# A two-layer gated-convolution, pooling and gating decoder step with experts: gate products ordered further ahead of their branch, small TensorE steps moved between blocks, another prologue and another item head

## The reference

```python
for i in range(2):
    xn = rmsnorm(x, norm_mix_g[i])
    z = xn @ w_in[i]                       # 8 x 256 mixer columns, then 4 x 1024 gate columns
    br_a = B(z) * conv3(C(z) * h(z))
    br_b = silu(layernorm(conv31(cfa(z) * sigmoid(cfb(z))) + bias))
    br_c = (pool_2_4_8_16(zp) - zp) @ pool_w * scale
    br_d = u(z) * (tril(sgu_w) @ layernorm(v(z)) + sgu_b)
    proj = [br @ w_branch[i, n] for n, br in enumerate((br_a, br_b, br_c, br_d))]
    x = x + (sum(sigmoid(gate_n(z)) * proj[n] for n in range(4))) @ w_out[i]
    xn = rmsnorm(x, norm_ffn_g[i])
    x = x + (swiglu(xn) if i == 0 else top2_of_8_swiglu_experts(xn))
    x = x + sigmoid(rmsnorm(x, norm_ple_g[i]) @ ple_w_gate[i]) * (p[i] @ ple_w_proj[i])
y = rmsnorm(x, final_norm_g)
```

## Time and profile before

| | us |
|---|---|
| median of 3 runs | 5181.46 (5172.38 to 5184.09) |
| the profiled execution | 5169.23 |
| its span, first to last instruction | 5167.6 |
| PE busy | 4955.4 (96%) |
| DVE busy | 3402.1 (66%) |
| ACT busy | 1598.1 (31%) |
| POOL busy | 402.1 (8%) |
| mean granted clock of TensorE | 0.975 |

### The profile page before, as it was taken

How to read it: one execution, slowest core, us unless ns; L and a number is a source line. 1 busy time by engine, 2 the same in 40 slices (tenths; PEclk the granted TensorE clock), 3 DMA queues, 4 the chain that set the end, 5 groups by cost and what they waited for, 6 DMA issues and landing times. The chain is left out here.

```text
span 5167.6 us, 86722 instructions
## 1 busy us (share of the span) xinstructions
PE 4955.4 (96%) x33128; PEld 4885.8 (95%) x33129; DVE 3402.1 (66%) x5297; ACT 1598.1 (31%) x2280; POOL 402.1 (8%) x246
## 2 busy tenths in 40 slices
PE   8999999999998999999969999999999999999979
PEld 7999999999998999999959999999999999999968
DVE  5677756445546656776556776666667887876665
ACT  2111222111112311122224444333334444443333
POOL 3111101101012021111010000000000000000020
PEclk8999999999999999999979999999999999999979
DMA  2111111111111111111035554444445555554431
GB/s 96 51 38 39 43 48 33 50 42 47 41 49 43 42 45 50 40 41 46 31 114 170 179 170 167 156 146 148 159 154 196 194 191 181 199 176 155 146 124 42
DMA packets 398927, 527.51 MB, mean 102 GB/s; under 512 B 12056, under 2 KB 353606, under 8 KB 398616
## 3 DMA queue, kind: packets, MB, share of 16 engines
q1 hardware_dynamic: 359552, 460.75, 26.7%
q0 software_dynamic: 11136, 33.97, 2.0%
q10 hardware_dynamic: 27928, 28.60, 1.7%
HBM read 494.87 MB, written 28.39 MB: 101 GB/s over the span
## 5 line engine op out<-in xcount | busy, mean ns | idle before, releaser
L1522 DVE TENSOR_TENSOR WLO<-WRAW,WHI 128x1024 fp32r<-128x1024 f32 x866 | 1065.7, 1232 | 316.3 <-ACT WHI L1138 189.7
L661 PE MATMUL PS<-XHI,WHI 128*128 128x384 f32 (+1 forms) x3648 | 1201.8, 329 | 0.6 <-DVE XLO L1749 0.3
L663 PE MATMUL PS<-XHI,WLO 128*128 128x384 f32 (+1 forms) x3648 | 1196.8, 328 | 0.0
L662 PE MATMUL PS<-XLO,WHI 128*128 128x384 f32 (+1 forms) x3648 | 1196.3, 328 | 0.0
L1138 ACT ACTIVATE WHI<-WRAW 128x1024 fp32r<-128x1024 f32 x866 | 898.9, 1051 | 885.4 <-PE PS L767 610.4
L661 PE MATMUL PS<-XSH,WHI 128*128 128x232 f32 (+6 forms) x3584 | 1059.8, 296 | 24.6 <-DVEq L2201 21.3
L662 PE MATMUL PS<-XSL,WHI 128*128 128x232 f32 (+6 forms) x3584 | 1057.0, 295 | 0.0
L663 PE MATMUL PS<-XSH,WLO 128*128 128x232 f32 (+6 forms) x3584 | 1055.5, 295 | 0.0
L661 PEld LDWEIGHTS PS<-XSH,WHI 128*128 128x128 f32 x3584 | 681.5, 190 | 26.7 <-DVE EACC L2249 22.9
L661 PEld LDWEIGHTS PS<-XHI,WHI 128*128 128x128 f32 x3648 | 690.7, 189 | 2.8 <-DVE XLO L1749 1.0
L662 PEld LDWEIGHTS PS<-XLO,WHI 128*128 128x128 f32 x3648 | 690.7, 189 | 0.7
(11 more groups left out here) (367 smaller groups left out, 5775.7 us busy)
## 6 DMA issues: line engine op xcount, KB each, us to landing
WRAW<-in_moe_w_gate SPq DMA_DIRECT2D x112, 1024.0 KB, 4.9
WRAW<-in_moe_w_up SPq DMA_DIRECT2D x112, 1024.0 KB, 4.9
WRAW<-in_moe_w_down SPq DMA_DIRECT2D x112, 1024.0 KB, 4.9
WRAW<-in_w_in SPq DMA_DIRECT2D x48, 1024.0 KB, 5.2
WRAW<-in_ffn_w_gate SPq DMA_DIRECT2D x11, 1024.0 KB, 5.1
WRAW<-in_ffn_w_up SPq DMA_DIRECT2D x11, 1024.0 KB, 5.2
WRAW<-in_ffn_w_down SPq DMA_DIRECT2D x11, 1024.0 KB, 4.8
XG<-sorted_rows POOLq DMA_DIRECT2D x18, 512.0 KB, 4.9
```

The costliest lines, as they stand in the source:

```text
L661: pe.matmul(PS[:, bank, 0:n], wh, hi(k), start=(k == 0), stop=False)
L662: pe.matmul(PS[:, bank, 0:n], wh, lo(k), start=False, stop=False)
L663: ins = pe.matmul(PS[:, bank, 0:n], wl, hi(k), start=False, stop=(k == KC - 1))
L1522: v.do(dve.tensor_tensor(WLO[s][:], raw_view(conv.n // 2 % RAW, conv.n % 2, kind), WHI[s][:].bitcast(F32), ALU.subtract), conv)
```

## The change

1. **Gates ahead.** In the first of the eight steps of every `gate_project`, TensorE computes the gates of all three blocks, then waits for the branch, then computes the three branch products. DVE and ACT follow: three gate tiles T[0] to T[2], then three additions. The other seven steps stay alternating.
2. **Small steps behind a block.** `column_unit` and `gate_project` take a list `between`. State stores, channel sums, pool weights, the transposes of p (layer 0), `stats` and `spread` stand behind the first or second block of a unit instead of ahead of it or behind the whole of it.
3. **Waits by slice and block.** Where a unit follows newly split activations, it waits for each slice of each block. The split of XNEW at the end of layer 0 is in 24 pieces, block by block, instead of 8.
4. **Prologue.** The gain rows are issued by ACT's queue and transposed ahead of everything. The squares are no longer added in the bank-wise order: ACT squares the token rows of XIN with a running sum into RTOK (nine operations of 1024 elements), after the first two conversions. `stats()` is left out for layer 0's first norm. The first unit waits for a block's evictions and not for the sums; the spread follows the first block of the second unit.
5. **Item head.** The first unit of an item waits slice by slice and stands ahead of the aligned address; a second unit at 336 tokens follows behind it, and then the jump. The bodies begin with the third unit.

```diff
-        def column_unit(HI, LO, first_use=None, after_first=lambda: None):
-
-            use()
+        def blocks_of(HI, LO, splits=None, between=()):
+
             slot = unit.n % HL
-            for t0, n in BLOCKS:
+            for j, (t0, n) in enumerate(BLOCKS):
                 b = open_bank()
                 product(b, n, slot, lambda k: HI[:, k, t0:t0 + n], lambda k: LO[:, k, t0:t0 + n],
-                        first_use if t0 == 0 else None).then_inc(q.next(), 1)
-                if t0 == 0:
-                    after_first()
+                        (lambda k: splits(j, k)) if splits else None).then_inc(q.next(), 1)
+                if j < len(between):
+                    between[j]()
...
+            for d in range(KC):
+                use()
+                slot = unit.n % HL
+                if d == 0:
+                    blocks_of(XHI, XLO, splits, between)
+                    pe.wait_ge(S[ready], count)
+                    pe.wait_ge(S["pw_lo"], pw.n + 1)
+                    for t0, n in BLOCKS:
+                        branch(t0, n)
+                else:
                     for t0, n in BLOCKS:
                         b = open_bank()
                         product(b, n, slot, lambda k: XHI[:, k, t0:t0 + n], lambda k: XLO[:, k, t0:t0 + n]).then_inc(q.next(), 1)
...
-            stats()
-            column_unit(XHI, XLO, first_use=(W_MIX1 if l else None))
-            spread()
-            column_unit(XHI, XLO)
+            if l:
+                column_unit(XHI, XLO, splits=lambda j, k: W_MIX1 + KC * j + k + 1, between=(stats, spread))
+                column_unit(XHI, XLO)
+            else:
+                use()
+                slot = unit.n % HL
+                for j, (t0, n) in enumerate(BLOCKS):
+                    pe.wait_ge(S["evicted"], KC * (j + 1))
+                    b = open_bank()
+                    product(b, n, slot, lambda k: XHI[:, k, t0:t0 + n], lambda k: XLO[:, k, t0:t0 + n]).then_inc(q.next(), 1)
+                unit.n += 1
+                column_unit(XHI, XLO, between=(spread,))
...
-            states_out(GLU, YB, PB)
-            gate_project("br_d", l + 1, U_SPLIT)
+            gate_project("br_d", l + 1, U_SPLIT, between=(lambda: states_out(GLU, YB, PB),))
...
+            column_unit(XHI, XLO, between=(channel_sums,))
...
-            states_out(ZP, YP, PC)
-            gate_project("br_b", l + 1, YB_SPLIT)
+            column_unit(XHI, XLO, between=(spread,))
+            gate_project("br_b", l + 1, YB_SPLIT, between=(lambda: states_out(ZP, YP, PC),))
...
+            gate_project("br_c", l + 1, YP_SPLIT, between=(pool_weights,))
...
                             if first and u == 0:
-                                spread()
+                                column_unit(XHI, XLO, splits=lambda j, k: W_FFN - 3 * KC + 3 * k + j + 1, between=(stats, spread))
...
                     nc.switch_bb("item_announced")
+                    splits = hs.n
+                    hs.n += KC
+                    gate_up(CAP, lambda k: hs.at(splits + k + 1))
                     pe.addr_align(256, offset=0, max_nops=0)
-                    pe.wait_ge(S["split_done"], hs.take(KC))
                     gate_up(CAP)
...
-                            left = item(rows, 1, fetch_next)
+                            left = item(rows, 2, fetch_next)
...
+            if l == 0:
+                last_down = W_FFN + 6 * FFN_GROUPS
+                gate_project("p_ready", 1, P_SPLIT, splits=lambda j, k: last_down + 3 * k + j + 1,
+                             between=(lambda: (p_columns(), stats()), spread))
+            else:
+                p_columns()
+                gate_project("p_ready", 2, P_SPLIT, splits=lambda j, k: hs.at(hs.n + min(6 * j + 6, 2 * NT)), between=(stats, spread))
...
+        act.wait_ge(S["rtok_clear"], 1)
+        for block, (t0, n) in enumerate(BLOCKS):
+            tiles = range(t0 // P, -(-(t0 + n) // P))
+            act.wait_ge(S[f"x_loaded{block}"], 16 * len(tiles))
+            for j in tiles:
+                w = tokens(j)
+                act.activation(XIN[0:w, j, :], XIN[0:w, j, :], ACT.Square, accum_out=RTOK[0:w, j:j + 1]).then_inc(S["row_squares"], 1)
+        convert()
...
             for d in range(KC):
                 convert()
                 if merge and 1 <= d <= MERGE_EARLY:
                     merge_low(d - 1)
-                for j, (t0, n) in enumerate(BLOCKS):
+                if d == 0:
+                    three = [gates(d, j, br_pulls) for j in range(3)]
+                for j in range(3):
                     if j == 2 and d < KC - 1:
                         split_pw()
...
+                    add_branch(d, j, *(gates(d, j, br_pulls) if d else three[j]))
```

More of the change, by code:

```diff
@@ L698, in _, with gate_project, branch @@
         sq, diag = Count(), Count()
-        def gate_project(ready, count, Y, after_first=lambda: None):
-            pe_ready = [False]
-            for j in range(4):
-                for h in range(2):
-                    use()
-                    slot = unit.n % HL
+        def gate_project(ready, count, Y, splits=None, between=()):
+            def branch(t0, n):
+                b = open_bank()
+                wh, wl = PWH[pw.n % 2], PWL[pw.n % 2]
+                for k in range(2):
+                    pe.matmul(PS[:, b, 0:n], wh[:, k, :], Y[0][:, k, t0:t0 + n], start=(k == 0), stop=False)
+                    pe.matmul(PS[:, b, 0:n], wh[:, k, :], Y[1][:, k, t0:t0 + n], start=False, stop=False)
+                    ins = pe.matmul(PS[:, b, 0:n], wl[:, k, :], Y[0][:, k, t0:t0 + n], start=False, stop=(k == 1))
+                ins.then_inc(q.next(), 1)
+            for d in range(KC):
[8 more added lines that the diff above has]
+                else:
                     for t0, n in BLOCKS:
@@ L869, in _, with pool_weights @@
-            gate_project("br_c", l + 1, YP_SPLIT)
+            column_unit(XHI, XLO, between=(spread,))
+            gate_project("br_b", l + 1, YB_SPLIT, between=(lambda: states_out(ZP, YP, PC),))
+            def pool_weights():
+                pe.wait_ge(S["pooled"], l + 1)
+                pe.wait_ge(S["pbd_loaded"], 64 * (l + 1))
+                for c in range(2):
+                    for t0, n in BLOCKS:
+                        b = misc_bank()
+                        pe.matmul(PS[:, b, 0:n], PBD[:, c, :], YP[:, c, t0:t0 + n], start=True, stop=True).then_inc(m.next(), 1)
@@ L1482, in _ @@
                         act.activation(x, x, ACT.Copy, scale=gain(6)[:, d:d + 1]).then_inc(S["xnew_ready"], 1)
+                for j, (t0, n) in enumerate(BLOCKS):
+                    if j == 2 and d < KC - 1:
+                        split_pw()
+                    sigmoid(n, d, j)
+                    q.n += 2
+                    if d:
+                        squares(t0, n)
+                if d == 0:
+                    for t0, n in BLOCKS:
+                        squares(t0, n)
             if l == 0:
-                for d in range(KC):
-                    act.wait_ge(S["split_req"], split.at(split.n + 1))
-                    act.activation(XHI[:, d, :], XNEW[:, d, :], ACT.Copy).then_inc(split.next(), 1)
+                for t0, n in BLOCKS:
+                    for d in range(KC):
+                        act.wait_ge(S["split_req"], split.at(split.n + 1))
+                        act.activation(XHI[:, d, t0:t0 + n], XNEW[:, d, t0:t0 + n], ACT.Copy).then_inc(split.next(), 1)
         norm_sqrt()
@@ L1753, in _ @@
                 dve.sem_inc(S["sgu_zeroed"], 1)
-            norm()
+                norm()
+            else:
+                norm_rows()
+                diagonals()
+                convert()
+                spread_rstd()
             v.do(dve.memset(MV[:], 1.0))
@@ L2347, in _ @@
                     v.sync()
-                    split_x(d, j, x, low=False)
+                    return x
+                if d == 0:
+                    three = [gates(d, j) for j in range(3)]
+                    whole = []
+                    for j in range(3):
+                        if j == 2:
+                            split_pw()
+                        whole.append(add_gated(j, *three[j]))
+                    for j in range(3):
+                        split_x(d, j, whole[j], low=False)
+                else:
+                    for j in range(3):
+                        if j == 2 and d < KC - 1:
+                            split_pw()
+                        gate = gates(d, j)
+                        finish_x()
+                        split_x(d, j, add_gated(j, *gate), low=False)
             finish_x()
```

219 lines of the change are left out of this document (104 added, 115 removed).

## The result

The changed kernel takes 5144.59 us (median of 4 runs, 5142.14 to 5149.72); the kernel before took 5182.77 us on the same chip (5172.38 to 5188.36). The ratio is 0.993, 95% interval 0.9912 to 0.9948: faster by 36 us (38 by the medians). The forecast was 68 us, 5113 us with a range from 5085 to 5138. The sign was right, the size was half, and the time lies above the range.

What follows compares the result with a forecast made beforehand. TensorE, busy 96% of the span, bounds the kernel; only its idle time or lower clock can yield. Terms 14 + 27 + 3.3 + 5 + 1 - 1 + 18.6 = 68 us, so 5181.5 - 68 = 5113 us, range 5085 to 5138.

Steps and rivals of the forecast that it cites:

- prologue: Start of the kernel: first product at 31.0 us instead of 44.98, a gain of 14 us (9 to 19).
- small steps and gates ahead: Mixers, both layers: waits at state stores, branches, channel sums and pool weights covered, plus clock: 27 us together.
- FFN entry: Statistics wait goes behind the first block: 3.3 us gained (1 to 6).
- the layer embedding of layer 0: A gate block moves into the wait for copies of P, and a low-half weights wait is covered: 5 us (3 to 9).
- entry to layer 1: Split of x in 24 pieces: gain of 3 us against a delay of 2 to 5, -1 us (-4 to 2).
- item heads: Slice waits at seven heads: 15.5 us of idle and 7.5 of clock, less 4.4 for the wider unit; 18.6 (8 to 26).
- last layer embedding: Layer embedding of layer 1: 1.5 us of waits go, the clock may fall once; +1 us (-2 to 3).
- So I put no new stall there: First unit of gate stages: about 13 us of DVE work against 15 of TensorE, six banks for six results, so no stall.
- Rival 2: Mixers: DVE becomes the bound and the removed pauses reappear as waits for banks; 5145 us, chance 0.06.
- Rival 4: Prologue and heads gain nothing, as first weights or gain rows land late and the clock stays low; 5146 us, chance 0.03.
- A later head is entered with only 1.61 us of idle, so between 0 and 1.6 us of that work can come out: Item heads: size reading and jump hidden under the data wait may show, taken as 0.7 x 7 = 5 us.
- rivals 1 and 3: Code loading at item heads: 1, seven idle 3.3 us each, 5136 us, chance 0.13; 3, dearer, slower than before, chance 0.02.

Runs made afterwards that it cites:

- split_early: Changed kernel with DVE's split of the second step's branch weights moved right behind the three gates, ahead of the additions: 5123.46 us, ratio 0.9892.
- one_unit: Changed kernel with one unit in the item head, behind the aligned address as before the change, but waiting slice by slice: 5146.09 us, ratio 0.9938.
- no_align_down: split_early without the aligned address ahead of the last down projection of every item: 5114.2 us, ratio 0.9869.
- noalign_only: Changed kernel without the aligned address ahead of the last down projection of an item, DVE's order kept: 5126.92 us, ratio 0.9906.
- head_before: Changed kernel with the whole old item head: one unit behind the aligned address and one wait for all eight slices: 5146.10 us, ratio 0.9946.
- no_aligns: no_align_down with the aligned address between the item head's first and second unit left out as well: 5122.39 us, ratio 0.9895.
- alternating: no_align_down with each gate stage's first step back to gates and branch in turn, small steps left behind the first block: 5158.11 us, ratio 0.9963.

## Why the prediction was right or wrong

The forecast's terms, within the traces: prologue 15.4 us for 14, small steps and gates ahead 4.2 for 27, FFN entry and the layer embedding of layer 0 11.1 for 8.3, entry to layer 1 -1.3 for -1, item heads -12.2 for 18.6, last layer embedding 1.0 for 1; 1.3 us more came in the router, where none was forecast. Two terms failed.

- *Prologue:* right, in the place of the first product (29.57 us for 31.0) and in the main in what sets it; that TensorE waits 2.42 us for the last tokens wasn't foreseen.
- *Small steps and gates ahead:* the waits named in the earlier trace rows vanished. The step that failed is "So I put no new stall there". I compared DVE's 13 us with TensorE's 15 and six banks with six results, but didn't ask which of DVE's operations the *next* step needs first, and the split for it stood behind them all. The sum of work was right, the order in it cost most of 25.4 us and the clock behind it. split_early shows it. That the same short operation takes 2.7 to 3.7 us during a scaling on POOL, which is part of three of the waits, isn't in the forecast either.
- *Rival 2* has nearly the measured number (5145) with another mechanism, and that is luck: no bank was waited for, and the same work of DVE in another order took most of the waits away. Rival 4 has 5146, and the prologue, which it gives up, gained 15.4 us.
- *FFN entry, layer embedding, entry to layer 1:* 9.7 us from the second row of the table to the start of layer 1's stage, for 7.3 forecast (3.3 + 5 - 1): about as sized.
- *Item heads:* two steps failed. "A later head is entered with only 1.61 us of idle, so between 0 and 1.6 us of that work can come out" took the shortest head for all. one_unit, which leaves the head behind its jump and takes only the slice waits, idles 1.5 to 3.5 us at every head and gains 0.6 us in all. The change escapes that by moving the unit ahead of the aligned address, whose worth I hadn't seen: of the 21.3 us at seven heads 15.0 went in the changed kernel, partly behind late pages, and 11.3 in no_align_down, for 15.5 forecast (the forecast's own numbers, 20 less 0.7 x 7, give 15.1). And the term lacked the last down projection: I looked for late code only at the heads (rivals 1 and 3), where the jump indeed became short, while the other aligned address of the same bodies lost 23.1 us in the profiled execution. noalign_only shows its size as 18 us by medians.
- *The sum:* with both stalls out, no_align_down takes 5114.2 us, where 5113 was forecast; by its ratio 5181.46 x 0.9869 = 5114. That doesn't bear out the sum. The removed aligned address isn't part of the forecast and was not tried in the kernel before, and within the traces the gain is 52.8 us over the whole span for 68, since the profiled execution of before was a quick one: 12.3 and 9.5 us in the mixers for 13.5 each, 10.7 in the items for 18.6, and -2.8 in the last layer embedding for +1. The near agreement of the medians is partly chance.
- *Open:* why a page is asked for in time in one execution and late in the next; why the kernel before shows none of these waits in its one trace and head_before one. The page comes 3.1 to 6.6 us ahead of the product in seven of the eight items of the kernel before and 1.8 to 2.9 in the changed one's four items without the wait. That bodies shorter by a unit move a page's end nearer to the aligned address fits this, but was only argued.

## What to carry to other kernels

When products are reordered so that one engine runs further ahead, list for the engine behind it what the next step wants first, and put that ahead of the bulk; equal sums of work say nothing. A wait's named releaser is the last one by time, and another may end just before it: before a wait is priced, ask what else ends there, and try its removal alone. Look at the length of a late operation as well as at its place, and at what the other engines do meanwhile. In code with jumps and aligned addresses, look at every aligned address of a body that changes its length, not only at the one that is edited, and take more than one profile, since late code comes and goes.

## What was not expected of the hardware

- The jump at an aligned address, one branch on TensorE's sequencer, lasted 5.3 to 6.0 us where its code page's packet (about 1 us) came after the work had ended, and 0.3 to 1.2 us elsewhere; TensorE idled 4.7 to 6.1 us for it. The same kernel had four of these waits in one execution and two in another.
- Left out, the aligned address at the last down projection took the 23 us of waits away, with none of them in any of four profiles (no_align_down, noalign_only, no_aligns, alternating), and 18 us of the time; left out at the head as well, it cost 8 to 13 us.
- The same jump at an item's head lasted 0.9 to 1.8 us with the unit behind it (before, head_before, one_unit), and under 0.5 us in the changed kernel, where 24 products stand ahead of it.
- The split of the branch weights on DVE, an operation of 0.42 us, took 2.6 to 3.8 us in 24 of the 25 cases in which it began during POOL's scaling of weights (3.6 to 4.0 us), and ended 0.3 us behind it.
